# The third block of a fused three-block kernel: bias tables turned one pattern a slot, row tiles turned early, gated rows stored a slot later, heads in turn

## What is computed

```python
h = jnp.einsum('btd,de->bte', x, w_in) + b_in
q_a, k_a, v_a, g_a, q_h, z_fwd, z_bwd, i_h, g_h = jnp.split(h, split_at, axis=-1)
o_a = neighbourhood_attention(heads_a(q_a), heads_a(k_a), heads_a(v_a), rpb)  # 8 heads of 64
o_a = o_a * jax.nn.silu(g_a)
o_fwd = hgrn2_chunk_scan(qh, k_f, ih, logf_f)                                 # 4 heads of 128
o_bwd = flip(hgrn2_chunk_scan(flip(qh), flip(k_b), flip(ih), flip(logf_b)))
o_h = rms(o_fwd + o_bwd) * hg_norm_gain * silu(g_h)
y = jnp.einsum('bte,ed->btd', concat([o_a, o_h]), w_out) + b_out
return layer_norm(DEEPNORM_ALPHA * x + y)
```

## Time and profile before

| | |
|---|---|
| time, median of 3 runs | 4561.35 us (4556.19 to 4565.02) |
| the profiled execution, its own time | 4560.75 us |
| its span | 4558.9 us |
| granted TensorE clock, mean | 0.969 |
| PE busy | 4255.9 us, 93% |
| DVE busy | 2695.0 us, 59% |
| ACT busy | 1808.8 us, 40% |
| third block | from 2906 us to the end; its slots 0 to 143 run from 2915 to 4217 us |

### The profile page before, as it was taken

How to read it: one execution, slowest core, us unless ns; L and a number is a source line. 1 busy time by engine, 2 the same in 40 slices (tenths; PEclk the granted TensorE clock), 3 DMA queues, 4 the chain that set the end, 5 groups by cost and what they waited for, 6 DMA issues and landing times.

```text
span 4558.9 us, 62157 instructions
## 1 busy us (share of the span) xinstructions
PE 4255.9 (93%) x24340; PEld 3457.5 (76%) x24372; DVE 2695.0 (59%) x4207; ACT 1808.8 (40%) x3435; POOL 654.2 (14%) x305
## 2 busy tenths in 40 slices
PE   7999999999899989999899979888999999899689
PEld 4888888889788877788677758767887777777467
DVE  5688888871566533044467667466354564376665
ACT  5111111111566631122466547455353453266453
POOL 2111111110333311111022112322000000000111
PEclk9999999999999999999999989999999999999789
DMA  4111111122544421111589862577664655654653
GB/s 170 51 51 51 51 51 51 51 72 91 188 131 128 129 92 49 65 59 63 188 259 290 272 255 93 177 226 257 221 206 166 198 185 169 205 188 150 207 188 129
DMA packets 515372, 663.95 MB, mean 146 GB/s; under 512 B 60348, under 2 KB 407296, under 8 KB 491658
## 3 DMA queue, kind: packets, MB, share of 16 engines
q1 hardware_dynamic: 466046, 576.89, 38.8%
q10 hardware_dynamic: 49036, 83.09, 4.9%
HBM read 442.24 MB, written 217.65 MB: 145 GB/s over the span
## 4 chain that ended last, share of the span: by engine, by line
PE 81%; DMA 6%; DVE 5%; SPq 3%; ACT 3%; issue 2%; POOL 1%; ACTq 0%; DVEq 0%; POOLq 0%
PE ps L226 10%; PE ps L227 10%; PE ps L228 10%; PE ps L3624 3%; PE ps L3625 3%; PE ps L3626 3%; PE ps L251 3%; PE ps L252 3%; PE ps L253 3%; PE ps L3744 2%; DMA w_split_tiles<-w 1%; PE ps L3713 1%; PE ps L239 1%; PE ps L240 1%; PE ps L241 1%
## 5 line engine op out<-in xcount | busy, mean ns | idle before, releaser
L226 PE MATMUL ps<-hh,wsplit 128*128 128x512 f32 x2048 | 821.7, 401 | 8.2 <-DVE hl L1376 4.2
L227 PE MATMUL ps<-hl,wsplit 128*128 128x512 f32 x2048 | 809.7, 395 | 0.0
L228 PE MATMUL ps<-hh,wsplit 128*128 128x512 f32 x2048 | 808.6, 395 | 0.0
L952 DVE SCALAR_TENSOR_TENSOR conv_acc<-conv_in,pcol,conv_acc 128x1024 f32<-128x1024 f32 x480 | 687.4, 1432 | 14.8
L226 PEld LDWEIGHTS ps<-hh,wsplit 128*128 128x128 f32 x2048 | 387.1, 189 | 102.3 <-issue 7.4
L227 PEld LDWEIGHTS ps<-hl,wsplit 128*128 128x128 f32 x2048 | 390.8, 191 | 91.7 <-issue 4.3
L228 PEld LDWEIGHTS ps<-hh,wsplit 128*128 128x128 f32 x2048 | 389.3, 190 | 89.3
L218 POOL TENSOR_TENSOR wsplit<-wraw,wsplit 128x1024 fp32r<-128x1024 f32 x72 | 204.9, 2856 | 1341.1 <-ACT wsplit L213 1341.1
L3624 PE MATMUL ps<-h_hi,w 128*128 128x512 f32 x896 | 374.9, 418 | 4.4 <-DVE h_lo L3422 4.4
L3625 PE MATMUL ps<-h_lo,w 128*128 128x512 f32 x896 | 357.7, 399 | 0.0
L3626 PE MATMUL ps<-h_hi,w 128*128 128x512 f32 x896 | 356.3, 398 | 0.0
(11 more groups left out here) (389 smaller groups left out, 8871.4 us busy)
## 6 DMA issues: line engine op xcount, KB each, us to landing
w<-w_split_tiles SPq DMA_DIRECT2D x108, 1024.0 KB, 5.4
wraw<-in_w_in SPq DMA_DIRECT2D x72, 512.0 KB, 3.8
w_split_tiles<-w SPq DMA_DIRECT2D x36, 1024.0 KB, 6.5
sh<-hy_ak ACTq DMA_DIRECT2D x48, 512.0 KB, 3.9
g_tiles<-b_ost SPq DMA_DIRECT2D x80, 256.0 KB, 5.5
w_raw<-in_w_in SPq DMA_DIRECT2D x36, 512.0 KB, 4.3
wo_raw<-in_w_out SPq DMA_DIRECT2D x32, 512.0 KB, 5.5
sh<-hy_ad ACTq DMA_DIRECT2D x32, 512.0 KB, 9.5
```

The lines of the kernel that those rows point to most:

```text
L226: e.matmul(p[:, :], wh, c.HH[tb][:, k, :], start=k == 0, stop=False)
L227: e.matmul(p[:, :], wh, c.HL[tb][:, k, :], start=False, stop=False)
L228: t = e.matmul(p[:, :], wl, c.HH[tb][:, k, :], start=False, stop=k == 7)
L952: e.scalar_tensor_tensor(v, a[:, h * 1024 + j:(h + 1) * 1024 + j], c.convw(j, ch), v, ALU.mult, ALU.add) \
```

## The change

It has four parts, all in the third block.

1. `bias`: the three patterns of a table are flipped in three slots (9, 10, 11 plus 6pr) in place of one, on PE and DVE; the store follows in slot 12+6pr in place of 11+6pr.
2. `turn_x`: at slots 36, 72 and 108, the first two of the four row tiles are turned at the end of the slot before, behind its unit and ahead of its `post` steps. This holds for all engines, so SP issues the load of tiles 2 and 3 there too.
3. `att_st`: SP's store of gated rows becomes a step of its own behind the unit of slot s+3; DVE's `att_o` stays where it was.
4. `val`: the loop over key groups is now the outer one and that over the two heads the inner one.

```diff
+            after(s + 3, "att_st", L.avs.index((v, a)))
...
-        after(9 + 6 * pr, "bias", pr)
-        after(11 + 6 * pr, "bias_st", pr)
+        for pat in range(3):
+            after(9 + 6 * pr + pat, "bias", pr, pat)
+        after(12 + 6 * pr, "bias_st", pr)
...
         if s in L.begin:
-            L.order += [("turn_x", 4 * (s // 36) + j) for j in range(4)]
+            L.order += [("turn_x", 4 * (s // 36) + j) for j in range(2 if s else 0, 4)]
...
+        if s + 1 in L.begin:
+            L.order += [("turn_x", 4 * ((s + 1) // 36) + j) for j in range(2)]
         L.order += sorted(post.get(s, []), key=lambda x: 30 if x[0] == "el" else rank.get(x[0], 20))
...
-        elif k == "att_o":
+        elif k == "att_st":
             w = s[1]
             v, a = L.avs[w]
             e.wait_ge(*c.by_dve["att_o", w])
...
-        for hh in range(2):
-            for i, g in enumerate(gs):
-                o = 256 * (w % 2) + 64 * j
+        o = 256 * (w % 2) + 64 * j
+        for i, g in enumerate(gs):
+            for hh in range(2):
                 t = e.matmul(c.P[4][64 * hh:64 * hh + 64, o:o + 64], L.V[:, v % 2, 4 * (g - g0) + j, 64 * hh:64 * hh + 64],
```

More of the change, by code:

```diff
@@ L3401, in state, with bias @@
                 e.scalar_tensor_tensor(to, now, L.dec[:, n % 4, j:j + 1], u, ALU.mult, ALU.add).then_inc(*done)
-    def bias(pr):
+    def bias(pr, pat):
         bt = L.BT[:, pr % 2, :].rearrange("p (t i x) -> p t i x", t=3, x=32)
-        if pr >= 2:
+        if pr >= 2 and pat == 0:
             e.wait_ge(*L.bd_st[pr % 2][pr - 2, 1])
[L3407 to L3413, removed]
+        e.wait_ge(*L.b_pe[pr, pat])
+        e.tensor_tensor(bt[:, pat, :, :], v3(L.ab["flip", pr, pat][:, 0:384], 32), L.win[:, pat, :].unsqueeze(1).to_broadcast([128, 12, 32]), ALU.add) \
+            .then_inc(*c.by_dve.up(("flip", pr, pat)))
+        e.wait_ge(*c.by_dve["flip", pr, pat])
+        e.tensor_tensor(flat(L.V[:, pr % 2, 0:9, :]).rearrange("p (t i x) -> p t i x", t=3, x=32)[:, pat, :, :], bt[:, pat, :, :],
+                        L.rwin.unsqueeze(2).to_broadcast([128, 12, 32]), ALU.add).then_inc(*L.b_dve.up((pr, pat)))
     for s in L.order:
@@ L3453, in b3_dve @@
         elif k == "bias":
-            bias(s[1])
+            bias(*s[1:])
         elif k == "qk":
@@ L3729, in b3_pe @@
         elif k == "bias":
[L3730 to L3735, removed]
+            pr, pat = s[1:]
+            if pat == 0:
+                e.wait_ge(*L.c_ld["rwin"])
+                e.wait_ge(*L.t_ld[pr % 2][pr, 1, 3, 2])
+            p = take_bank(e, c, ("flip", pr, pat), L.ab)
+            e.matmul(p[:, 0:384], L.flip, L.BT[:, pr % 2, 384 * pat:384 * pat + 384], start=True, stop=True).then_inc(*L.b_pe.up((pr, pat)))
         elif k == "qk":
```

## The result

The changed kernel takes 4536.45 us, the median of 4 runs (4532.88 to 4538.82), against 4558.77 us for the kernel before in runs beside it (4554.48 to 4565.02). The ratio is 0.9944, with a 95% interval of 0.9932 to 0.9956. I had forecast 4537 us. The profiled execution took 4538.82 us, 21.9 less than that of before; its span is 4537.0 us.

A forecast was written before the change was run, and what follows sets the result against it. PE was taken as the bound, busy for 93% of the span, with SP's weights' chain setting the pace in slots 0 to 35. 6 + 13 + 0 + 5 = 24 us off 4560.75 gave 4536.8, forecast as 4537 us, range 4529 to 4545.

The forecast's parts named there:

- The flips' waits: PE's four waits for a third flip's bank, 18.2 us: removed, but only 1.3 us arrive at slot 36.
- the store's move: Tables' store issued behind the next table's loads on SP: saves 2.0 us for each of three pairs, net 4.8 us.
- slot 36's first unit about 6 us earlier plus 4: Sign in the profile after: 6 us earlier at slot 36, plus 4 for its row tiles.
- The charge of 0.4 us: Cost per pair set against the store's move: tables queued ahead of a raw load delay it by 0.4 us.
- raw loads that land late behind a table's store: Sign that the forecast is wrong, in SP's queue: part 1 would then be worth nothing.
- The row tiles: Slots 36, 72 and 108: unit 4.3 us earlier, three times, 13 us; bounds 4.5 and 20 in all.
- the 5.94 us from tile 2 to the unit: PE's time from tile 2 to slot 72's first matmul, kept at 5.94 us; 4.2 only in the upper bound.
- I take half: Heads in turn, passes of `val`: second head starts one pass-time late, so 5 us of at most 10.
- Only the row tiles: Rival: parts 1 and 4 do nothing, the weights' chain stays where it is; 4547.8 us, chance 0.18.
- the flips in full: Rival: the flips' 18.2 us of waits are won in full; 4524.6 us, chance 0.12.
- The rows are late as before: Rival: part 2 gives only its low bound, 4.5 us, the rest as forecast; 4545.3 us, chance 0.08.
- A change of head costs a pass: Rival: each of 448 more head changes on PE costs 0.11 us, 49 us; slower, 4591 us, chance 0.05.

The follow-up runs named there:

- the two groups of kernels: Kernels with the tables' store in slot 11+6pr against slot 12+6pr; SP's last raw load issued 270.9 to 273.6 us against 266.1 to 269.1 us after unit 0.
- part 1 alone: Kernel before with only the flips in three slots and the tables' store in slot 12+6pr, run twice: ratios 0.9991 and 0.9985.
- p2_turns: Kernel before with only the row tiles' change (two turned early, with their row loads): ratio 0.9963, median 4545.75 us.
- rows_late: Changed kernel, but SP loads row tiles 2 and 3 where it did before, behind the weight loads: ratio 0.9966 to the kernel before, median 4544.87 us.
- p3_store: Kernel before with only the store of gated rows moved behind the unit of the slot: ratio 1.0002, median 4563.88 us.
- p4_heads: Kernel before with only the two heads taken in turn: ratio 0.9976, median 4552.68 us.
- p1_flips: Kernel before with only the flips in three slots and the store in slot 12+6pr, first run: ratio 0.9991, median 4558.70 us.

## Why the prediction was right, step by step

**The flips' waits (1.3 us of 18.2).** Right in kind and size. 16.5 of the 18.2 us came back, at line 3668 as forecast and at the unit behind the flips. For the store's move, forecast at 4.8 us net, the two groups of kernels show 4.7 at the chain's end, but part of that agreement is luck, as the next paragraph shows. The whole part was forecast at 6 us and measured 4 and 7 us, and 5.5 between the means of unit 0 to 35. The sign "slot 36's first unit about 6 us earlier plus 4" did not come out in the profiled pair: it is 6.1 us earlier in all, counted from unit 0.

The charge of 0.4 us for a raw load behind the tables was mis-sized. Of the changed kernel, SP's timeline around pair 0's store, the median landing of what was issued from 3022.5 to 3031 us, and a split on ACT:
```profile
3022.75 0.40 SPq L2822 DMA_DIRECT2D w_raw<-in_w_in  x1
...
3025.90 1.25 SPq L2982 DMA_DIRECT2D bias_rows<-att_v  x1
3029.48 0.38 SPq L2822 DMA_DIRECT2D w_raw<-in_w_in  x1
...
3038.63 0.38 SPq L2822 DMA_DIRECT2D w_raw<-in_w_in  x1
...
w_raw<-in_w_in SPq DMA_DIRECT2D x2, 512.0 KB, 5.4
...
3036.12 1.06 ACT L2843 ACTIVATE w<-w_raw 128x1024 fp32r<-128x1024 f32 x1 [1.79 <-DMA w_raw<-in_w_in]
```
ACT's split waits for the load that was issued at 3029.48 and landed 6.6 us later, at 3036.1; the corresponding one of before, issued at 3029.61, took 4.1. Counted from unit 0, SP's raw loads stood 2.3 us ahead of before at the first two of these, and 0.2 behind at the third (3038.63 - 2917.56 = 121.1 against 120.9). So behind pair 0 the tables took 2.5 us (2.3 + 0.2), not 0.4. By the prediction's own sign, raw loads that land late behind a table's store, part 1 should then have been worth nothing; it was not. The chain made part of it up again: its last load is 1.8 us ahead of before in the changed kernel (269.1 against 270.9), and 3.5 and 4.8 in the two executions of part 1 alone. How it does so, and what makes these differ, stays open.

**The row tiles (13 us).** Right in mechanism, too small by a quarter: 16.6 us in the three stretches, 17 us in the median of `p2_turns`. Two terms were mis-sized. The rows' landing was taken as 4.1 us and was 3.3, so tile 2 no longer waited. And the 5.94 us from tile 2 to the unit were taken over as they were; they are now 3505.87 - 3501.05 = 4.82. I had seen that the transposes ran slower after the wait and put that only into the bound. The granted clock says why. Windows of before (columns: the window and its length, busy time and instructions of PE, PEld, DVE, ACT and POOL, PEclk, DMA share, GB/s):
```profile
3502.00:3506.00 4.00, 2.69 (x25) 1.97 (x24) 1.97 (x4) 2.36 (x5) 0.00 (x0) 1.00 0.99 332
3510.90:3513.00 2.10, 1.94 (x8) 1.57 (x8) 0.28 (x1) 0.66 (x2) 0.00 (x0) 0.50 0.59 219
3513.00:3517.00 4.00, 2.07 (x9) 1.57 (x9) 2.48 (x4) 2.65 (x4) 0.00 (x0) 0.50 0.00 0
3517.00:3520.00 3.00, 3.00 (x7) 2.35 (x8) 0.00 (x0) 0.37 (x1) 0.00 (x0) 0.50 0.00 0
3520.00:3530.00 10.00, 10.00 (x45) 8.20 (x45) 0.98 (x2) 1.26 (x2) 0.00 (x0) 0.99 0.34 120
```
and of the changed kernel:
```profile
3501.00:3502.50 1.50, 1.07 (x9) 0.86 (x8) 0.63 (x3) 0.83 (x3) 0.00 (x0) 1.00 0.84 320
3503.00:3505.00 2.00, 1.16 (x8) 0.84 (x8) 1.15 (x3) 1.13 (x2) 0.00 (x0) 1.00 0.98 401
3505.80:3508.00 2.20, 2.13 (x9) 1.81 (x10) 0.00 (x0) 0.48 (x1) 0.00 (x0) 1.00 0.91 302
```
Before, PE stood 5.29 us for the rows and its clock was granted at 0.50 afterwards, the lower of its two levels (1.2 GHz), for about 9 us; the full level came back when the unit had run 3 us. In the changed kernel it stays at 1.00 here. Besides the two tiles this shortens the unit itself: 24 matmuls took 7.19 us before (from 3516.90 to 3524.09) and 5.68 after. That is another 1.5 us, which lies in the next stretch of the table; I had no term for it. In `rows_late`, where the wait is back, both tiles need 1.94 and 1.97 us again.

All this is slot 72. At the two other places the tiles ran at the full level too, but the clock still fell for 3.4 us at the start of the unit, though no wait there was over 1.6 us. At slot 108 of the changed kernel, whose unit starts at 3827.47:
```profile
3827.70:3830.90 3.20, 3.20 (x8) 2.44 (x8) 0.00 (x0) 0.00 (x0) 0.00 (x0) 0.50 0.82 301
```
So the unit took 8.25 us before and 7.00 after at slot 36, but 7.30 and 7.20 at slot 108. A shorter wait does not by itself keep the clock up, and what the unit gains differs from place to place.

**The store (0 us).** Right: 1.0002. The 140.0 us went in part to the gate's load (74.5 us in the changed kernel, 74.6 in `p3_store`), in part to the weight loads that wait for PE, and the time did not change. As forecast, all 13 waits of the gate's load lie in the last row block.

**The heads (5 us).** The step that failed is "I take half". It is the upper bound: a step of 12 passes takes the 0.57 us worked out for a lone head with three groups, and a pair of steps 0.92 where that working gave 0.93. With 32 of each that is 32 x 0.16 + 32 x 0.16 = 10 us, and 11 were measured. Changing heads after each two passes does not cost the second head a pass-time: its first pass starts 0.01 us behind the first head's. The Trainium skill's rule that a load overlaps a matmul only in other row groups ("TensorE: Matmul & The Clock Gate", Part 3, "The mechanism") is not borne out here, where the two heads share all rows and 12 passes fell from 0.73 to 0.57 us; the Trainium skill's rule that tiles run on their own ("TensorEngine Tiling (Array Packing)", "Key Properties") is. In the changed kernel only part arrived: 7.1 us between units 72 and 107, but 0.9 between 108 and 143, where the longest wait for v went from 10.9 to 12.9 us. With the heads alone (`p4_heads`) the same stretches took 307.6 and 356.5 us, 4.9 and 4.0 less than before.

**The sum.** Forecast 6 + 13 + 0 + 5 = 24, measured alone 4 + 17 - 1 + 11 = 31, together 22. Two terms were too small by 4 and 6 us, and together the parts gave some 9 us less than alone. But each ratio is uncertain by 4 to 6 us, and a difference made of five of them by some 11 or more, so a loss between the parts is not shown. The profiled pair has two places that would count toward it, 2.0 us more in the longest wait for v and 2.6 more behind slot 143; the stretch behind slot 143 took 345.3 to 350.1 us in the executions here, whatever the kernel, so the second is not shown to belong to the change. The forecast of 4537 lies nearer to 4536.45 than its terms deserve: that is luck.

**The rivals.** "Only the row tiles" fails by p4_heads, "the flips in full" by p1_flips. "The rows are late as before" became true only when `rows_late` put them behind the weights. "A change of head costs a pass" had the wrong sign.

## What to carry to other kernels

Where a wait is found to move rather than to vanish, find the chain that sets the pace there and look at what stands in its queue: here four times 24 small loads cost some 20 us, more than all four parts together moved in that stretch. In a queue that moves large tiles, the load that PE needs next goes ahead of those that it needs three slots later. And a long wait of PE has a price behind it too: cost the work after it at the clock that the profile shows for it, and look in the new profile whether that has gone with the wait.

## What the runs showed of the hardware

- Two heads' passes in two column tiles of 64 that share all rows run beside each other if they alternate, 0.01 us apart: 12 passes in 0.57 us, as long as the 6 of one head were worked out to take, against 0.73 us with one head after the other.
- A wait of 5.29 us was followed by some 9 us at a granted clock of 0.50, in which 8 transposes took 1.94 in place of 1.06 us. With no wait over 1.6 us at the three places it stayed at 1.00 at slot 72, but was at 0.50 for 3.4 us at slots 36 and 108.
- The same load of 512 KB landed after 3.3 us ahead of two weight tiles and, in `rows_late`, after 7.2 us behind them.
- 24 small loads kept SP for 15.4 us, 0.64 us each.
